# A float32 transformer block: the first adaptive-norm weights split by columns, with the first v products between the two parts

## What is computed

```python
def ada_modulate(x, c, norm_g, ada_w, ada_b):
    ada = jax.nn.silu(c) @ ada_w + ada_b
    shift, scale, gate = jnp.split(ada, 3, axis=-1)
    h = rmsnorm(x, norm_g) * (1.0 + scale[:, None, :]) + shift[:, None, :]
    return h, gate[:, None, :]
...
    h, gate_res = ada_modulate(x, c, norm_g, ada_w, ada_b)
    a, u, v, gate = _split(h @ in_w, EVEN_SIZES)
```

## Time and profile before

| | |
|---|---|
| median of 3 runs | 985.36 us (984.07 to 986.63) |
| the profiled execution | 985.16 us, its span 983.4 us |
| TensorE busy | 951.5 us, 97% of the span |
| VectorE, ScalarE busy | 713.7 us (73%), 508.8 us (52%) |
| chain of waits that ended last | 88% TensorE, 7% VectorE, 2% DMA |
| first v product starts, v3 ends | 34.45 us, 56.9 us |

### The profile page before, as it was taken

One profiled execution on the slowest core, in us unless ns is written; L12 is line 12 of the kernel. 1 busy time (PEld: TensorE's weight loads), 2 busy tenths in 40 slices (PEclk: granted clock), 3 DMA queues, 4 the chain that ended last, 5 costly groups with the idle time before them and its releaser, 6 DMA issues.

```text
span 983.4 us, 17238 instructions
## 1 busy us (share of the span) xinstructions
PE 951.5 (97%) x7025; PEld 875.3 (89%) x7025; DVE 713.7 (73%) x994; ACT 508.8 (52%) x745; POOL 40.9 (4%) x68
## 2 busy tenths in 40 slices
PE   6999999999999999999999999999999999999998
PEld 5799989989899889999778889889998978898987
DVE  4778877767957946675998988967888765555554
ACT  4654364446645555644755456475555554444444
POOL 2100000000000013210100000000000000000000
PEclk9999999999999999999999999999999999999999
DMA  9998676846875877576577887774534457676631
GB/s 365 385 342 257 211 268 231 283 129 226 291 259 167 295 261 250 179 260 213 155 254 255 281 274 263 246 257 136 172 119 138 131 172 247 184 223 212 192 101 43
DMA packets 134247, 219.43 MB, mean 223 GB/s; under 512 B 8585, under 2 KB 100090, under 8 KB 134168
## 3 DMA queue, kind: packets, MB, share of 16 engines
q1 hardware_dynamic: 132416, 214.99, 66.3%
q0 software_dynamic: 992, 1.76, 0.7%
q10 hardware_dynamic: 760, 1.59, 0.4%
HBM read 217.25 MB, written 1.05 MB: 222 GB/s over the span
## 4 chain that ended last, share of the span: by engine, by line
PE 88%; DVE 7%; DMA 2%; issue 2%; ACT 1%; ACTq 0%; DVEq 0%
PE pw L568 62%; PE pacc L568 24%; DVE WL L1659 1%; DMA ring<-in_ada_w 1%; DVE SQT L1755 1%; DVE hl L1760 1%; PE pw L1021 1%; DMA cst<-in_consts 1%; DVE ACC L1675 1%; ACT hh L1174 1%; DVE AR L1675 0%; PE pw L997 0%; DVE xT L2059 0%; ACT WH L1174 0%; ACT SQT L1174 0%
## 5 line engine op out<-in xcount | busy, mean ns | idle before, releaser
L1174 ACT ACTIVATE WH<-ring 128x1024 fp32r<-128x1024 f32 x288 | 302.7, 1057 | 271.1 <-PE pw L568 171.7
L1659 DVE TENSOR_TENSOR WL<-ring,WH 128x1024 fp32r<-128x1024 f32 x288 | 348.3, 1224 | 84.2 <-ACT WH L1174 83.5
L568 PE MATMUL pacc<-YH,WH 128*128 128x256 f32 x672 | 192.8, 287 | 2.7 <-issue 1.7
L568 PE MATMUL pacc<-YH,WL 128*128 128x256 f32 x672 | 190.1, 283 | 0.0
L568 PE MATMUL pacc<-YL,WH 128*128 128x256 f32 x672 | 190.0, 283 | 0.0
L568 PE MATMUL pw<-hh,WH 128*128 128x256 f32 x704 | 186.7, 287 | 1.5 <-DVE WL L1659 0.8
L568 PE MATMUL pw<-hh,WL 128*128 128x256 f32 x704 | 183.9, 283 | 0.0
L568 PE MATMUL pw<-WH,hh 128*128 128x512 f32 x448 | 177.3, 396 | 2.8 <-DVE WL L1659 2.3
L568 PE MATMUL pw<-WL,hh 128*128 128x512 f32 x448 | 175.2, 391 | 0.0
L568 PE MATMUL pw<-hl,WH 128*128 128x256 f32 x704 | 142.6, 284 | 0.0
L568 PEld LDWEIGHTS pw<-hh,WH 128*128 128x128 f32 x704 | 134.8, 191 | 6.0 <-issue 5.7
(11 more groups left out here) (272 smaller groups left out, 778.2 us busy)
## 6 DMA issues: line engine op xcount, KB each, us to landing
ring<-in_w_mod SPq DMA_DIRECT2D x72, 512.0 KB, 4.7
ring<-in_odd_in_w SPq DMA_DIRECT2D x56, 512.0 KB, 5.8
ring<-in_ada_w SPq DMA_DIRECT2D x48, 512.0 KB, 6.9
ring<-in_ffn_w_gate SPq DMA_DIRECT2D x88, 256.0 KB, 3.3
ring<-in_ffn_w_up SPq DMA_DIRECT2D x88, 256.0 KB, 4.3
ring<-in_ffn_w_down SPq DMA_DIRECT2D x44, 512.0 KB, 4.6
ring<-in_even_in_w SPq DMA_DIRECT2D x40, 512.0 KB, 6.5
ring<-in_even_out_w SPq DMA_DIRECT2D x16, 512.0 KB, 5.6
```

The source lines that it names most:

```text
L568: return eng.matmul(o, a, b, start=start, stop=stop, skip_group_check=True)
L1174: return eng.activation(dst, src, func, **kw)
L1659: tt(WL[:, i % NL, :], slot(half_of(i)), WH[:, i % NH, :].bitcast(F32), SUB).then_inc(s_lo, 1)
```

## The change

The 16 first ada pieces are now 512 rows by 512 columns instead of 256 by 1024. The first eight (scale, then shift) give columns 0 to 511, which is what k tiles 0 to 3 of `h` need; the other eight give k tiles 4 to 7. Between them in the list stand v0 and v2, the two v units of the upper half of the depth; v1 and v3 follow after the last first-layer ada unit. On TensorE v0 and v2 run before the second scale and shift are complete, with half 11 between them; then come half 13, the second scale sum, half 14, the second shift sum, v1 and v3. The halves and sums of the second part use 32 moving columns instead of 128. TensorE has six ada halves instead of five, VectorE ten instead of eleven, each in two instructions of 512 columns; the last eight warming products are gone. `vc1` now stands ahead of half 3 and of `xt`. The first constants load is 256 columns instead of 128; the rest of the constants moves from ScalarE's queue to GpSimd's, where that queue now waits for piece 21 instead of 19; ScalarE's seven small loads move ahead of its first wait.

```diff
-ADA_PE = (1, 3, 6, 9, 12)
+ADA_PE = (1, 3, 6, 11, 13, 14)
...
-    units += ada(a0, 1, 2) + ada(a0, 0, 1)
+
+    def first(cc, q):
+        return [("ada", a0[512 * i:512 * i + 512, 1024 * cc + 512 * q:1024 * cc + 512 * q + 512].rearrange(
+            "(k p) n -> p k n", p=P), 4, 512) for i in range(2)]
+
+    def v_half(j):
+        half_k(f"v{j}", ew, 512 * (j % 2), 2048 + 512 * (j // 2))
+
+    units += first(1, 0) + first(0, 0)
+    v_half(0)
+    units += first(1, 1)[:1]
+    v_half(2)
+    units += first(1, 1)[1:] + first(0, 1)
     at = len(units)
-    for j in range(4):
-        half_k(f"v{j}", ew, 512 * (j % 2), 2048 + 512 * (j // 2))
+    v_half(1)
+    v_half(3)
...
-    for key, ms in (("p0", (0, 2, 4)), ("p1", (5, 7)), ("p2", (8, 10)), ("p3", (11,)), ("p4", (13, 14, 15))):
-        for m in ms:
-            at.setdefault(key, []).append(("half", m))
...
+        def first_bank(c, q):
+
+            return f2(pacc[:, 4 * q + 2 * c:4 * q + 2 * c + 2, :])
+
+        def first_acc(c, q):
+            return (ACC[:, :], ACC2)[c][:, 512 * q:512 * q + 512]
...
+            def ada_half(m, n=P):
+
+                c, q, r, g = m // 4 % 2, m // 8, m % 4, 2 * ada_units[m // 2] + m % 2
                 p.wait_ge(s_silu, 1)
                 p.wait_ge(*landed(g))
-                for j in range(8):
-                    last = mm(pacc[:, j, c * P:c * P + P], slot(g)[:, j * P:j * P + P],
-                              SIL[:, m % 8:m % 8 + 1].to_broadcast([P, P]), m == 1 and j % 2 == 0, False)
+                for j in range(4):
+                    for e in range(2):
+                        last = mm(first_bank(c, q)[:, j * P:j * P + n], slot(g)[:, 512 * e + j * P:512 * e + j * P + P],
+                                  SIL[:, 2 * r + e:2 * r + e + 1].to_broadcast([P, n]),
+                                  (c, q) not in begun and j == 0 and e == 0, False)
                 last.then_inc(s_adp, 1)
-
-            def ada_sum(c, js, name):
-                for j in js:
-                    last = mm(pacc[:, j, c * P:c * P + P], (ACC, ACC2)[c][:, j * P:j * P + P], ones, False, True)
+                begun.add((c, q))
...
+            def ada_sum(c, q, name, n=P):
+                for m in (8 * q + 4 * c + 3, 8 * q + 4 * c + 2, 8 * q + 4 * c + 1):
+                    p.wait_ge(*ada_done(m))
+                for j in range(4):
+                    last = mm(first_bank(c, q)[:, j * P:j * P + n], first_acc(c, q)[:, j * P:j * P + P], ones[:, 0:n],
+                              False, True)
...
+            ada_half(3)
+            ada_sum(0, 0, "ada0a")
+            p.wait_ge(d_x, 16)
+            turn(XN, "xt")
...
-            ada_sum(0, range(8), "ada0")
             pb = open_("dt")
             p.wait_ge(s_lam, 1)
             close(eng.transpose(pb[:, 0:16], DTR, ident[0:16, 0:16]), "dt")
-            p.wait_ge(*gone["ada0"])
-            ada_half(9)
-            ada_half(12)
+            ada_sum(1, 0, "ada1a")
             warm(8, "warm0a")
-            p.wait_ge(*ada_done(15))
-            ada_sum(1, range(4), "ada1a")
-            ada_sum(1, range(4, 8), "ada1")
-            warm(8, "warm0c")
-
-
-            cols_N(L_EVEN, "v")
+
+
+            bks = [open_(f"v{j}") for j in range(4)]
+            wide(L_EVEN, "v0", bks[0:2], 0)
+            ada_half(11, 32)
+            wide(L_EVEN, "v2", bks[2:4], 0)
+            ada_half(13, 32)
+            ada_sum(0, 1, "ada0", 32)
+            ada_half(14, 32)
+            ada_sum(1, 1, "ada1", 32)
+            wide(L_EVEN, "v1", bks[0:2], 4)
+            wide(L_EVEN, "v3", bks[2:4], 4)
+            for j in range(4):
+                full[f"v{j}"] = used(f"v{j | 1}")
+            p.wait_ge(d_cst, 16)
...
+            eng.dma_start(cst[:, 0:2 * P], I["consts"][:, 0:2 * P]).then_inc(d_id, 16)
             eng.dma_start(XN, I["x"].rearrange("o (a p) n -> p (o a) n", p=P)).then_inc(d_x, 16)
+            pack_loads(eng.dma_start, 1, d_vec[1])
             eng.preload_act_table_set("exp_and_others")
             s.wait_ge(*gone["vc0"])
             act(sil_e[:, 0:8], col("c", 0, 8), ACT.Exp, scale=-1.0).then_inc(s_sil, 1)
             act(sil_e[:, 8:16], col("cond", 0, 8), ACT.Exp, scale=-1.0).then_inc(s_sil, 1)
-            pack_loads(eng.dma_start, 1, d_vec[1])
-            eng.dma_start(cst[:, P:], I["consts"][:, P:]).then_inc(d_cst, 16)
...
-            for k in range(8):
-                s.wait_ge(*gone[f"xr{k // 2}"])
-                act(SQT[:, k, :], SQT[:, k, :], scale=GS[:, k:k + 1]).then_inc(s_u, 1)
...
+            def scaled(ks):
+                for k in ks:
+                    s.wait_ge(*gone[f"xr{k // 2}"])
+                    act(SQT[:, k, :], SQT[:, k, :], scale=GS[:, k:k + 1]).then_inc(s_u, 1)
+
+            s.wait_ge(s_gs, 1)
+            scaled(range(4))
             cut(-AHEAD_H)
             s.wait_ge(s_mod, 2)
-            s.wait_ge(s_u, 8)
             modulate(L_EVEN, M0[:, 0:8], range(4))
-            cut(1 - AHEAD_H)
+            cut(3 - AHEAD_H)
+            s.wait_ge(s_gs, 2)
+            scaled(range(4, 8))
+            cut(4 - AHEAD_H)
...
+            def first_half(m):
+
+                g, acc = 2 * ada_units[m // 2] + m % 2, first_acc(m // 4 % 2, m // 8)
+                v.wait_ge(*landed(g))
+                for e in range(2):
+                    src, wc = slot(g)[:, 512 * e:512 * e + 512], SIL[:, 2 * (m % 4) + e:2 * (m % 4) + e + 1]
+                    if m % 4 == 0 and e == 0:
+                        a = ts(acc, src, wc, None, MUL)
+                    else:
+                        if e == 0:
+                            v.wait_ge(s_ada, ada_done(m)[1] - 1)
+                        a = stt(out=acc, in0=src, scalar=wc, in1=acc, op0=MUL, op1=ADD)
+                    if e == 0:
+                        v.wait_ge(*v.step(a))
+                    else:
+                        a.then_inc(s_ada, 1)
...
+            first_half(0)
+            first_half(2)
...
+            first_half(4)
             v.wait_ge(*gone["vc1"])
-            first_add(0, 8, 0, 8, "ada0")
-            v.wait_ge(*gone["ada0"])
-            stt(out=GS, in0=M0[:, 8:16], scalar=1.0, in1=col("norm_g", 0, 8), op0=ADD, op1=MUL).then_inc(s_gs, 1)
+            first_add(0, 0, "ada0a")
+            first_scale(0)
             mods[0] += 1
-            ada("p3")
+            v.wait_ge(s_x2, 2)
+            rsqrt(RS[:, 0:2], RS[:, 6:8], 1.0 / D, RS[:, 2:4], RS[:, 4:6])
+            first_half(5)
+            first_half(7)
             v.wait_ge(*gone["dt"])
             tt(RS[:, 32:48], col("lam_re", 0, 16), DTC, MUL).then_inc(s_lam, 1)
-            ada("p4")
-            first_add(1, 0, 0, 4, "ada1a")
+            first_add(1, 0, "ada1a")
             cut(-AHEAD_L)
             v.wait_ge(s_mod, 2)
-            v.wait_ge(s_u, 8)
             first_lows(range(4))
-            first_add(1, 4, 4, 4, "ada1")
-            cut(1 - AHEAD_L)
+            cut(2 - AHEAD_L)
+            first_half(8)
+            cut(3 - AHEAD_L)
+            first_half(9)
+            first_half(10)
+            first_half(12)
+            first_add(0, 1, "ada0")
+            first_scale(1)
+            first_half(15)
+            first_add(1, 1, "ada1")
+            cut(4 - AHEAD_L)
...
-            g.wait_ge(*landed(19))
+            g.wait_ge(*landed(21))
+            eng.dma_start(cst[:, 2 * P:], I["consts"][:, 2 * P:]).then_inc(d_cst, 16)
```

More of the change, by code:

```diff
@@ L527, in urs @@
             return last
-        full, gone, place = {}, {"ada0": (s_mod, 1), "ada1": (s_mod, 3)}, {}
+        full, gone, place = {}, {"ada0": (s_mod, 3), "ada1": (s_mod, 4)}, {}
         block = ctx.enter_context(nc.Block())
@@ L762, in _ @@
             ada_half(1)
-            ada_half(3)
             def turn(x, name):
@@ L773, in turn @@
                     close(last, f"{name}{q}")
-            p.wait_ge(d_x, 16)
-            turn(XN, "xt")
             pb = open_("vc1")
@@ L786, in _ @@
             turn(XR, "xr")
-            p.wait_ge(*ada_done(7))
-            p.wait_ge(d_cst, 16)
-            ada_sum(0, range(8), "ada0")
             pb = open_("dt")
@@ L1267, in v_squares @@
                     yield
-            for j in range(4):
+            for j in (0, 2, 1, 3):
                 pieces(f"v{j}")
@@ L1771, in update, with first_add, first_scale @@
                 v.wait_ge(s_x, X_FIN[L] + 8)
-            def first_add(c, to, j0, n, name):
-                v.wait_ge(*full[name])
-                tt(MOD[:, to:to + n].unsqueeze(2), pacc[:, j0:j0 + n, c * P:c * P + 1],
-                   col("ada_b", to, n).unsqueeze(2), ADD).then_inc(s_mod, 1)
+            def first_half(m):
[13 more added lines that the diff above has]
+                        a.then_inc(s_ada, 1)
+            def first_add(c, q, name):
+                to = 8 - 8 * c + 4 * q
+                v.wait_ge(*full[name])
+                tt(MOD[:, to:to + 4].unsqueeze(2), v3(first_bank(c, q), 4)[:, :, 0:1],
```

(32 more changed lines are left out.)

5 lines of the change are left out of this document (1 added, 4 removed).

## The result

| | before | after |
|---|---|---|
| median | 984.72 us (4 runs, 984.06 to 986.63) | 996.5 us (4 runs, 995.28 to 998.33) |
| ratio, 95% interval | | 1.0111 (1.0097 to 1.0125) |
| profiled execution, its span | 985.16, 983.4 us | 998.33, 996.6 us |
| v0 starts, v3 ends | 34.45, 56.9 us | 32.64, 69.2 us |

The change makes the kernel 11.8 us slower; I had said 6.6 (992.0 against 985.4), with 996.0 as the upper end. In the profiled pair the difference is 13.2 us. Of that 12.3 are there when v3 ends, and 0.9 comes behind it: a wait of 0.95 at unit eg6, and one low stretch of the clock in each trace, at 507.9 us before and at 150.2 after.

What follows compares the result with a forecast made beforehand. TensorE, busy 97% of the span, bounds the kernel. To 985.16 us come 4.1 for v3's later end, 1.7 for a clock drop and 0.95 for eg6's wait: 991.9, forecast 992.0 us, range 986.8 to 996.

Steps and rivals of the forecast that it cites:

- The opening's chain: Steps from the first constants load through vc1, half 3, xt and scalings: v0 starts at 28.85 us, 5.6 earlier.
- half 3 to 16.3, the sum 0.9 to 17.2: Opening, behind vc1: half 3 ends at 16.3 us and its sum, taking 0.9, at 17.2.
- The idle time and the drop ahead of v0: TensorE idles 2.4 us ahead of v0, then some 3.2 us run at half speed, losing 1.7 us.
- my argument from the earlier trace: At v0: 2.2 us of idle at 505.7 had lowered the clock, 1.7 us at 212.5 had not; so a drop.
- rival (a): The clock stays at 2.4 GHz over the idle time ahead of v0: 990.3 us; chance 0.22.
- The price of 32 columns: Ada halves and sums of the second part: 1.8 us for a half, 0.9 for a sum, 0.11 a record.
- rival (c): Not slower: 32-column products cost in proportion to their columns; 986.9 us with the clock kept; chance 0.10.
- rival (b): Low clock also in the opening (2.4 us) or at v1 (1.7 more): 993.7 to 996 us; chance 0.20.
- From v2 to v3's end: v1 starts 7.0 us behind v2, 1.3 idle follows its first piece, v3 ends 19.35 us behind v2.
- eg6's wait: At the start of unit eg6, TensorE waits 0.95 us for WL, behind two VectorE halves moved to eg4.
- The sum: Whole kernel: 985.16 + 4.1 + 1.7 + 0.95 = 991.9, so 992.0 us; v3 ended near 62.7 us.
- The mis-sized term: Clock loss: one drop at the start of v0, some 3.2 us at half speed, 1.7 us lost.

Runs made afterwards that it cites:

- e1: The changed kernel with ada half 3 moved ahead of the vc1 transposes: 993.65 us, ratio 1.0076.
- e2: The changed kernel with ten more warming products in the idle time ahead of v0: 994.6 us, ratio 1.0096.
- e3: The changed kernel with 128 moving columns instead of 32 in the second part's ada halves and sums: 995.06 us, ratio 1.01.
- e5: The changed kernel with VectorE's ada halves 26 and 27 back at u3 instead of eg4: 999.06 us, ratio 1.0138.
- e6: The changed kernel with v1's cuts, ada half 15 and the table load moved ahead of the wait for the second scale sum: 996.86 us, ratio 1.0112.
- e10: The e9 kernel with the evacuation of v2's and v3's banks ahead of ScalarE's last WH cut there: 982.49 us, ratio 0.9977 to the kernel before.
- e7: The changed kernel with the edits of e1, e2 and e3 together: 992.56 us, ratio 1.0071.
- e9: On e5, e6, e7 edits with halves 13, 14 on VectorE: shift sum inside v2, half 13 and first WH earlier, fewer warming products; 984.68 us, ratio 0.9993.

## Why the prediction was right in its sign and short in its size

**The opening's chain: right, but for the clock.** vc1 at 13.98 us (13.8 forecast), held by the small loads as said. From there to `xt` I had 3.4 us; it took 6.5. The step that failed is "half 3 to 16.3, the sum 0.9 to 17.2", both priced at the high clock, behind a wait that I had just put there myself. Half 3 took 3.78 us and the sum 2.00; e1, without the wait, has 2.05 and 1.16. From `xt` to v0 I had 11.65 and it took 12.2.

**The idle time and the drop ahead of v0: right.** 2.34 us of idle (2.4 forecast), a low stretch behind it, and v0 to v2 in 14.4 us against 14.5 with the drop. e2 shows that the idle time causes it. The Trainium skill ("TensorE: Matmul & The Clock Gate", section "Why this matters for your kernels") advises against idle gaps over about 3 us; here 2.34 us ahead of v0 cost the clock in after, e1, e3, e5 and e6 alike, so the measurement decides: shorter ones can cost it too. But my argument from the earlier trace rows was weaker than it looked. The idle time of 2.3 us that had lowered the clock there lowers it in e5 too, and not in after or in e10. Nor is 1.7 us safe, as rival (a) took it: behind the 1.77 us in this line of after TensorE ran at 0.51; before, behind 1.77 us ahead of the same records, it stayed at 1.00.

```profile
149.80 0.35 PE L584 MATMUL pw<-YH,WH 128*128 128x256 f32 x1 [1.77 <-issue]
```

**The price of 32 columns: right.** 1.86 us for a half (1.8 forecast), 0.11 for a record; rival (c) is out. What I missed is that the clock can fall over such a passage: with 32 columns it fell in each trace that has one, with 128 in neither of two. I took these products for TensorE being busy (5.4 of 7.0 us), and priced the passage without a word on the clock except in rival (b).

**From v2 to v3's end.** v1 starts 8.3 us behind v2, 7.0 forecast; the rest takes 13.8 us, 12.35 forecast. The terms: 1.3 more for slow halves and sums, 2.5 more for v1's first piece at half speed, 1.3 less since this hides the idle time behind it. e3, with the clock up, has 7.3 and 12.6.

**eg6's wait: right.** 0.95 us forecast, and after shows, in TensorE's timeline:

```profile
133.41 0.35 PE L584 MATMUL pw<-hh,WH 128*128 128x256 f32 x1 [0.95 <-DVE WL L1692]
```

**The sum.** From 62.7 us for v3's end with one drop: 3.8 late at v0, 0.1 early over v0 and v2, 1.3 and 1.5 late behind them. That is 6.5, and 69.2 is what the trace has. Of it 1.1 are chains priced short (0.5 ahead of v0; behind v2 0.3 for v1's start and 0.25 for what follows, by e3), 0.2 is vc1's later start, and the other 5.2 are clock. **The mis-sized term is the clock: 1.7 us where it was 6.9**, 3.1 in the opening, 1.6 at v0 and 2.2 behind v2. Rival (b) named both further places and came true, and even it had them at 2.4 + 1.7 instead of 3.1 + 2.2; with the chains on top the median lies 0.5 us above my range. I had given it 0.20 as if it needed bad luck; yet the earlier trace rows already showed the first records slow, and the forecast itself put idle times behind them. In e2 and e3, with the same order of work there, `vc1` to `xt` takes 5.2 us instead of 6.5, so 1.3 of the 3.1 differ from one execution to another.

**What stays open.** Why the same idle time lowers the clock in one kernel and not in another. And the medians move less than the profiled v3's ends: 2.85 of 4.05 us in e1, 1.4 of 3.2 in e3, 3.9 of 7.7 in e7. Part of it can be told. Behind v3 the twelve traces differ in hardly more than two things: low stretches of 1.7 us each (none in e10, two in e5 and e6, one in the others) and the waits named above (0.95 or 0.4 us at the gate units, in e9 the 1.73 ahead of a0). With these taken off, span minus v3's end is 924.5 to 925.1 us in all twelve. So a median holds, beside the opening, how many low stretches its runs met. How many those were in the runs that weren't profiled stays open; the profiled run of after is the slowest of its four, 1.8 us above its median.
